# Moving the pieces of the modulation vectors between the stages of a three-block transformer kernel

## The chip, the cores and the metric

The kernel runs on one core of one Trainium2 chip. The metric is the device time of one execution in microseconds (us). Engines are named as in the profile: PE is TensorE, DVE is VectorE, ACT is ScalarE, POOL is GpSimd, SP is SyncE, which here does nothing but issue DMAs.

## The reference, cut to what matters

Two layers with a mixer and a feed-forward network (FFN) each, and then a second block (attention, cross attention, experts), all for 256 tokens of width 1024 in float32. What matters here is the modulation of the first two layers:

```python
def adaln_modulation(c, w, b):                     # w: 1024 x 6144, one per layer
    mod = jax.nn.silu(c) @ w + b
    return [m[:, None, :] for m in jnp.split(mod, N_MOD, axis=-1)]

for layer in range(DEPTH):                         # 2 layers
    shift_m, scale_m, gate_m, shift_f, scale_f, gate_f = adaln_modulation(c, *ada[layer])
    h = rmsnorm(x, pre_m) * (1.0 + scale_m) + shift_m
    x = x + gate_m * rmsnorm(mixers[layer](h), post_m)
    h = rmsnorm(x, pre_f) * (1.0 + scale_f) + shift_f
    x = x + gate_f * rmsnorm(swiglu(h, *ffns[layer]), post_f)
```

The modulations depend on the vector `c` alone, not on the tokens. They can be computed at any time before the place that uses them.

## The kernel before

**Stages.** The program is a list of stages, and every engine walks through it in the same order: `pro`, `proj0`, `ssd`, `mla` (the first layer's mixer), `ffn0`, `mix1`, `gla`, `nsa` (the second layer's mixer), `ffn1`, and then the second block (`mix2` to `experts`). Each engine has its own instruction stream, written out by hand in methods whose names begin with `pe_`, `ve_`, `se_`, `ge_`; the engines wait for each other on semaphores that count finished instructions of a stage.

**Projections.** A projection streams its weights from DRAM as slabs of 128x2048 float32 (1 MB), in a ring of three (`raw`). The products are made of three fp32r matmuls per 128x128 tile (lines 532 to 534; 528 to 530 where the tokens are the stationary side): each weight is split into a high part (`whi`, written by ACT, line 2127) and a low part (`wlo`, a subtraction on DVE or POOL, line 1203). The splits go by blocks of 1024 columns, half a slab, in a ring of three blocks: ACT may cut block j once PE is done with block j-3. `lo_engine` says who makes the low part: in the FFNs blocks with an even number are DVE's and odd ones POOL's; elsewhere in these stages all are POOL's. In `ffn0` DVE's is the first half of every slab. One call of `pe_linear` is one slab: 16 tiles in two halves (j = 0 and 1) of 24 matmuls. Next to it `ve_linear` does what DVE owes that projection, and cuts low parts up to two blocks ahead.

**An FFN** is eleven rounds of a gate slab, an up slab and the down slab of the round before (`pe_ffn`, `ve_ffn`). In each round DVE also multiplies silu(gate) by up (line 1562) and takes the low part of the product (line 1565).

**The modulation pieces.** The first four of the 24 column groups are done in the prologue. The other 80 pieces (list `ADA`: a piece is a quarter of a group of 512 columns) are spread over the program. `ve_ada` does one piece on DVE: it waits for the piece's 128x1024 float32 tile (512 KB, a ring of two, `ada_ring`) and adds its two halves, each times a scalar, to `ada_acc` (lines 1229 and 1232). Four pieces make a group. The call after the fourth one closes the group: there `pe_ada` waits for DVE's fourth piece and sums `ada_acc` over the partitions with four fp32 matmuls, eight records each time (line 617), and `ve_ada` waits for these, writes four columns of `mod_t` (line 1221), and then does its own next piece. Both engines count the calls (`ada_no`), so calls 4, 8, ... 80 close a group. Calls stand at the start of every `pe_linear`, `pe_linear_tok`, and every second column block of `pe_out`; with `eager=True` a projection has two, of which PE makes the second between the two halves of the slab, and DVE makes both before it cuts. `pe_ada` also notes (`ada_slab`) before which weight slab the next piece is loaded; SP issues all loads from one queue, and `sp_ada` waits there for the piece two before.

**Where the calls fall.** `proj0` has 12 (numbers 0 to 11), `ssd` 8, `mla` 8, `ffn0` 22 (28 to 49), `mix1` 5, `gla` 12 including the last `w_nq`, `nsa` 10 (67 to 76), `ffn1` four that do anything (77 to 80). `pe_ada_until` and `ve_ada_until` make up what is missing before a modulation is used; before the change they find nothing to do.

**`mix1` and `gla`.** After the first of four `w_gqk` projections DVE makes a gate and its running sums (four scans, line 1604). In `gla`, seven levels follow each other: DVE and ACT make factors (lines 1626 to 1654), PE a matmul per level (line 883), and between the levels PE fills its time with 11 projections (`FILLS`: 2, 2, 2, 1, 1, 1, 2).

Of the kernel before, what the change touches and what calls it, by code (L numbers as in the profile page):

```python
# [430 lines left out]
    return n, [slice(h0 + p, h0 + p + 2 * n - 1, 2) for h0 in range(0, nh, 2 * n) for p in range(2)]  # L431


ADA = [(0, g, q) for g in range(4, 12) for q in range(4)] + [(1, g, q) for g in range(12) for q in range(4)]


# [49 lines left out]
class Net:  # L486
# [26 lines left out]
    def tensor(self, e):  # L513
        e.wait_ge(self.landed["kc"], 16)
        for stage, run in (("pro", self.pe_pro), ("proj0", self.pe_proj0), ("ssd", self.pe_ssd), ("mla", self.pe_mla),
                           ("ffn0", self.pe_ffn0), ("mix1", self.pe_mix1), ("gla", self.pe_gla), ("nsa", self.pe_nsa),
                           ("ffn1", self.pe_ffn1), ("mix2", self.pe_mix2), ("moba", self.pe_moba), ("xa", self.pe_xa),
                           ("route", self.pe_route), ("gates", self.pe_gates), ("experts", self.pe_experts)):
            self.P.begin(stage)
            run(e)  # L520

    def pe_mm3(self, e, out, tile, xh, xl, start, stop, *keys, moving=False):
# [82 lines left out]
    def pe_ada(self, e):  # L605

        s = self.ada_no["P"]
        if s > len(ADA):
            return
        self.ada_no["P"] += 1  # L610
        self.ada_slab[s] = self.W.due()
        if s and ADA[s - 1][2] == 3:
            layer, g, _ = ADA[s - 1]
            e.wait_ge(*self.at("ada", s - 1))
            ps = self.banks.take(e, "ada", layer, g)
            for j in range(4):
                i = e.matmul(ps[:, j * 128:(j + 1) * 128], self.m.ada_acc[:, j * 128:(j + 1) * 128], self.m.ones, start=True,  # L617
                             stop=True, skip_group_check=True)
            i.then_inc(*self.P(("full", "ada", layer, g)))

    def pe_ada_until(self, e, layer, part):
        while self.ada_no["P"] <= ADA.index((layer, 2 * part + 1, 3)) + 1:
            self.pe_ada(e)
# [57 lines left out]
    def pe_proj0(self, e):  # L681
        m = self.m
        for i in range(3):
            self.pe_linear(e, "w_low", i, 8, 2, m.hH, m.hL, None if i else "mix0", eager=True)
        for i in range(6):
            self.pe_linear(e, "w_xbc", i, 8, 2, m.hH, m.hL)
            if i == 0:
                e.wait_ge(*self.at("low_squares"))
                self.pe_rstd(e, "qa", [range(0, 3)], m.tmp, lambda j: None)
                self.pe_rstd(e, "kva", [range(3, 5)], m.tmp, lambda j: None)  # L690
        e.wait_ge(*self.at("cs"))
        ps = self.banks.take(e, "dt_cs")
        for c in range(2):
            e.transpose(ps[:, 16 * c:16 * c + 16], m.dt[:, c * 128:(c + 1) * 128], m.kc("ident", 0, 16, 16))
            i = e.transpose(ps[:, 32 + 16 * c:48 + 16 * c], m.cs[:, c * 128:(c + 1) * 128], m.kc("ident", 0, 16, 16))
        i.then_inc(*self.P(("full", "dt_cs")))
# [119 lines left out]
    def pe_ffn(self, e, layer):  # L816
        m = self.m
        self.pe_ada_until(e, layer, 4)
        self.P.mark("end", f"mixer{layer}", "P")
        self.pe_norm(e, f"ffn{layer}", True)  # L820
        self.P.mark("sums", f"ffn{layer}", "P")
        for i in range(11):
            self.pe_linear(e, f"w_gate{layer}", i, 8, 2, m.hH, m.hL, None if i else f"ffn{layer}")
            self.pe_linear(e, f"w_up{layer}", i, 8, 2, m.hH, m.hL)
            if i:
                self.pe_down(e, layer, i - 1)
        self.pe_down(e, layer, 10)
        self.pe_post(e, f"ffn{layer}_post", layer, 5)
# [355 lines left out]
    def vector(self, e):  # L1184
        e.wait_ge(self.landed["kc"], 16)
        e.wait_ge(self.landed["pv"], 16)
        for stage, run in (("pro", self.ve_pro), ("proj0", self.ve_proj0), ("ssd", self.ve_ssd), ("mla", self.ve_mla),
                           ("ffn0", self.ve_ffn0), ("mix1", self.ve_mix1), ("gla", self.ve_gla), ("nsa", self.ve_nsa),
                           ("ffn1", self.ve_ffn1), ("mix2", self.ve_mix2), ("moba", self.ve_moba), ("xa", self.ve_xa),
                           ("route", self.ve_route), ("gates", self.ve_gates), ("experts", self.ve_experts)):  # L1190
            self.V.begin(stage)
            run(e)

    def cut_lo(self, e, X, upto):
# [14 lines left out]
    def ve_ada(self, e):  # L1209

        m, V = self.m, self.V
        s = self.ada_no["V"]
        if s > len(ADA):
            return
        self.ada_no["V"] += 1
        if s and ADA[s - 1][2] == 3:
            layer, g, _ = ADA[s - 1]
            c0 = 48 * layer + 4 * g
            ps = self.banks.tile("ada", layer, g)
            e.wait_ge(*self.at("full", "ada", layer, g))  # L1220
            e.tensor_tensor(out=m.mod_t[:, c0:c0 + 4], in0=ps[:, :].rearrange("p (a n) -> p a n", a=4)[:, :, 0],
                            in1=m.pv(f"ada_b{layer}", 4 * g, 4), op=ALU.add).then_inc(*V(("out", "ada", layer, g)))
        if s < len(ADA):
            _, _, q = ADA[s]
            e.wait_ge(self.ada_landed[s % 2], 16 * (s // 2 + 1))
            for k in range(2):
                c, w = m.silu_c[:, 2 * q + k:2 * q + k + 1], m.ada_ring[:, s % 2, k * 512:(k + 1) * 512]
                if q == 0 and k == 0:
                    e.tensor_scalar(out=m.ada_acc, in0=w, scalar1=c, scalar2=None, op0=ALU.mult).then_inc(*V())
                else:  # L1230
                    e.wait_ge(*V.last)
                    e.scalar_tensor_tensor(out=m.ada_acc, in0=w, scalar=c, in1=m.ada_acc, op0=ALU.mult,  # L1232
                                           op1=ALU.add).then_inc(*V(*([("ada", s)] if k else [])))
# [163 lines left out]
    def ve_proj0(self, e):  # L1397
        m, V = self.m, self.V
        e.memset(m.xb[:, :, 0:3], 0.0).then_inc(*V(("xb_zero",)))
        for i in range(3):  # L1400
            self.ve_linear(e, "w_low", i, 8, 2, eager=True)
            if i == 1:
                e.wait_ge(*self.at("out", "w_low", 1))
                e.tensor_scalar(out=m.dtx, in0=m.kp[0:16, :], scalar1=m.pv("dt_bias", rows=16), scalar2=None,
                                op0=ALU.add).then_inc(*V(("dt_raw",)))
# [137 lines left out]
    def ve_ffn(self, e, layer):  # L1543
        m, V = self.m, self.V
# [9 lines left out]
            e.wait_ge(*self.at("end", f"mixer{layer}", eng))  # L1554
        for i in range(11):
            s = slice(2 * (i % 2), 2 * (i % 2) + 2)
            self.ve_linear(e, f"w_gate{layer}", i, 8, 2)
            self.ve_linear(e, f"w_up{layer}", i, 8, 2)
            e.wait_ge(*self.at("out", f"w_gate{layer}", i))
            e.wait_ge(*self.at("full", f"w_up{layer}", i))  # L1560
            pu = self.banks.tile(f"w_up{layer}", i)[:, 0:512].rearrange("p (a t) -> p a t", a=2)
# [1498 lines left out]
```

## Time and profile before

| what | value |
|---|---|
| median of 3 runs | 2291.11 us (2288.9 to 2291.63) |
| the profiled execution | 2293.22 us, its span 2291.1 us |
| PE busy | 2033.5 us (89%) |
| DVE busy | 1311.9 us (57%) |
| ACT busy | 978.7 us (43%) |
| POOL busy | 1112.1 us (49%) |
| mean granted TensorE clock | 0.947 |

The stages stand in the trace at these times of the span: `proj0` from about 50 us, `ssd` from 131, `mla` from 192, `ffn0` from 292, `mix1` from 510, `gla` from 557, `nsa` from 714, `ffn1` from 850 to 1060. Busy time counts overlapping matmuls once; an idle stretch is given in brackets with what ended it. PEclk is the TensorE clock granted, as a share of full speed.

### The profile page before, as it was taken

Reading aid. Unit: us, or ns where it says so; the run is one execution under the profiler, and the core shown is the slowest. Engines: PE = TensorE matmul, PEld = TensorE weight load, DVE = VectorE, ACT = ScalarE, POOL = GpSimd, SP = SyncE. Lnnn points to the kernel's source line nnn. Section 1 sums busy time; section 2 is a strip of 40 time slices with the busy share of each in tenths; the row PEclk is TensorE's granted clock in tenths of the full one; section 3 lists DMA queues with packets and bytes.
Section 4 is the critical chain, followed back from the end, with each engine's and each line's share of the span. In section 5 each row is a group of like instructions: output and inputs, shape, how many; then the busy total and the mean of one; then the engine's idle time right before and its main releaser. Section 6 shows DMA issues by size and latency. Waiting matters only on the chain.

```text
span 2291.1 us, 38041 instructions
## 1 busy us (share of the span) xinstructions
PE 2033.5 (89%) x15708; PEld 1957.5 (85%) x15708; DVE 1311.9 (57%) x2049; ACT 978.7 (43%) x1433; POOL 1112.1 (49%) x506
## 2 busy tenths in 40 slices
PE   6688889987889769997988889767999999999998
PEld 6676789977877659997988879756899999999998
DVE  5788755537774764333823448999744444444444
ACT  5334354444333334444443545356334444444443
POOL 2452344445543233444856657866744444444443
PEclk8889899997889799999989989999999999999999
DMA  7542446644445234554434334322456555555543
GB/s 278 193 168 92 181 159 237 234 174 149 166 151 189 83 102 160 183 182 152 166 110 148 129 111 164 131 88 79 162 205 218 184 219 216 184 183 182 184 183 129
DMA packets 75915, 378.43 MB, mean 165 GB/s; under 512 B 6976, under 2 KB 24528, under 8 KB 38496
## 3 DMA queue, kind: packets, MB, share of 16 engines
q1 hardware_dynamic: 75744, 376.00, 45.6%
q8 instruction: 125, 2.05, 0.4%
q14 instruction: 46, 0.38, 0.0%
HBM read 366.54 MB, written 9.44 MB: 164 GB/s over the span
## 4 chain that ended last, share of the span: by engine, by line
PE 65%; DVE 20%; POOL 4%; ACT 3%; issue 2%; DMA 1%; DVEq 0%; SPq 0%; ACTq 0%
PE ps L532 19%; PE ps L533 18%; PE ps L534 18%; POOL wlo L1203 4%; DVE arena L1232 3%; PE ps L581 2%; DVE arena L1329 1%; DVE rs_t L2063 1%; DVE arena L1654 1%; DVE arena L2035 1%; PE ps L617 1%; ACT whi L2127 1%; PE ps L760 1%; DVE small L1317 1%; DVE arena L2063 1%
## 5 line engine op out<-in xcount | busy, mean ns | idle before, releaser
L1203 POOL TENSOR_TENSOR wlo<-raw,whi 128x1024 fp32r<-128x1024 f32 x387 | 979.2, 2538 | 1013.5 <-ACT whi L2127 1012.3
L532 PE MATMUL ps<-hhi,whi 128*128 128x256 f32 x2696 | 787.9, 292 | 70.7 <-POOL wlo L1203 30.5
L2127 ACT ACTIVATE whi<-raw 128x1024 fp32r<-128x1024 f32 x559 | 587.9, 1056 | 594.5 <-PE ps L534 470.9
L533 PE MATMUL ps<-hlo,whi 128*128 128x256 f32 x2696 | 778.4, 289 | 0.0
L534 PE MATMUL ps<-hhi,wlo 128*128 128x256 f32 x2696 | 777.4, 288 | 0.0
L532 PEld LDWEIGHTS ps<-hhi,whi 128*128 128x128 f32 x2696 | 533.6, 198 | 81.5 <-issue 49.9
L533 PEld LDWEIGHTS ps<-hlo,whi 128*128 128x128 f32 x2696 | 534.4, 198 | 0.1
L534 PEld LDWEIGHTS ps<-hhi,wlo 128*128 128x128 f32 x2696 | 533.5, 198 | 0.0
L532 PE MATMUL ps<-chi,whi 128*128 128x256 f32 x1600 | 457.6, 286 | 15.0 <-DVE clo L2091 7.2
L533 PE MATMUL ps<-clo,whi 128*128 128x256 f32 x1600 | 454.8, 284 | 0.0
L534 PE MATMUL ps<-chi,wlo 128*128 128x256 f32 x1600 | 454.7, 284 | 0.0
L1203 DVE TENSOR_TENSOR wlo<-raw,whi 128x1024 fp32r<-128x1024 f32 x172 | 217.4, 1264 | 396.9 <-ACT whi L2127 396.9
L532 PEld LDWEIGHTS ps<-chi,whi 128*128 128x128 f32 x1600 | 309.0, 193 | 19.3 <-issue 9.5
L533 PEld LDWEIGHTS ps<-clo,whi 128*128 128x128 f32 x1600 | 309.2, 193 | 0.0
L534 PEld LDWEIGHTS ps<-chi,wlo 128*128 128x128 f32 x1600 | 309.2, 193 | 0.0
L1232 DVE SCALAR_TENSOR_TENSOR arena<-arena,gs_t 128x512 f32<-128x512 f32 x140 | 181.1, 1294 | 14.6 <-DMA arena<-in_ada 5.8
L2584 ACT ACTIVATE rs_t<-ps 128x256 f32<-128x256 f32 x106 | 40.8, 385 | 164.7 <-PE ps L534 163.3
L581 PE MATMUL ps<-arena,kc_t 128*128 128x256 f32 x250 | 66.5, 415 | 27.4 <-ACT arena L2166 24.5
L2035 POOL TENSOR_TENSOR arena<-arena 128x512 f32<-128x512 f32 x48 | 72.4, 1511 | 30.7 <-PE ps L1157 15.4
L581 PEld LDWEIGHTS ps<-arena,kc_t 128*128 128x128 f32 x250 | 49.2, 206 | 41.5 <-issue 12.2
L1157 PE MATMUL ps<-rs_t,arena 128*128 128x128 f32 x344 | 49.1, 292 | 25.6 <-issue 11.5
L617 PE MATMUL ps<-kc_t,arena 128*128 128x128 f32 x160 | 29.6, 344 | 47.3 <-DVE arena L1232 45.7
(368 smaller groups left out, 2197.4 us busy)
## 6 DMA issues: line engine op xcount, KB each, us to landing
raw<-in_peer_down SPq DMA_DIRECT2D x64, 1024.0 KB, 4.8
raw<-in_peer_up SPq DMA_DIRECT2D x64, 1024.0 KB, 7.2
arena<-in_ada SPq DMA_DIRECT2D x80, 512.0 KB, 4.4
raw<-in_w_gate SPq DMA_DIRECT2D x22, 1024.0 KB, 4.9
raw<-in_w_up SPq DMA_DIRECT2D x22, 1024.0 KB, 4.9
raw<-in_w_down SPq DMA_DIRECT2D x22, 1024.0 KB, 4.8
arena<-in_ada SPq DMA_DIRECT2D x8, 1024.0 KB, 14.9
raw<-in_w_gab SPq DMA_DIRECT2D x8, 1024.0 KB, 4.7
```

The lines of the kernel that those rows point to most:

```text
L532: e.matmul(out, hi, xh, start=start, stop=False, skip_group_check=True)
L533: e.matmul(out, hi, xl, start=False, stop=False, skip_group_check=True)
L534: i = e.matmul(out, lo, xh, start=False, stop=stop, skip_group_check=True)
L581: i = e.matmul(ps[:, gi * 256:gi * 256 + T], self.m.ones, sq[:, j, :], start=n == 0, stop=n == len(tiles) - 1, skip_group_check=True)
L617: i = e.matmul(ps[:, j * 128:(j + 1) * 128], self.m.ada_acc[:, j * 128:(j + 1) * 128], self.m.ones, start=True, stop=True, skip_group_chec ...
L1157: t = e.matmul(ps[:, i * 128:(i + 1) * 128], m.oh1[:, n % 3, i * 128:(i + 1) * 128], m.oh2[n % 3][:, i * 128:(i + 1) * 128], start=True, s ...
L1203: e.tensor_tensor(out=lo, in0=w, in1=hi.bitcast(F32), op=ALU.subtract).then_inc(*X(("lo", j)))
L1232: e.scalar_tensor_tensor(out=m.ada_acc, in0=w, scalar=c, in1=m.ada_acc, op0=ALU.mult, op1=ALU.add).then_inc(*V(*([("ada", s)] if k else [])))
L2035: e.tensor_tensor(out=m.oh1[:, n % 3, :].rearrange("p (t a b) -> p t a b", t=4, a=8), in0=bc(ta[:, sl, :].unsqueeze(3), [128, 4, 8, 16]), ...
L2063: e.tensor_tensor(out=m.oh2[n % 3].rearrange("p (t n) -> p t n", t=4), in0=bc(m.iota.unsqueeze(1), [128, 4, 128]), in1=bc(m.pk[:, 2, 4 * n ...
L2127: e.activation(hi, w, ACT.Copy, scale=1.0).then_inc(*self.A(("hi", j)))
L2584: e.activation(m.ge[:, i, :] if i < NST else m.co[:, i % 2, :], self.banks.tile("expert", i)[:, 0:T], ACT.Gelu_apprx_tanh, scale=1.0).then ...
```

## The change

The calls are placed by stage. The first projection of the program (`w_low`, three slabs) has one call per slab and no longer two. Gate and up projections of both FFNs get two calls each. A limit by stage, `ADA_UPTO`, ends the calls in `mix1`, `gla` and `nsa` after number 72.

```diff
+ADA_UPTO = {"mix1": 72, "gla": 72, "nsa": 72}
 ...
             self.P.begin(stage)
+            self.ada_upto = ADA_UPTO.get(stage, len(ADA))
             run(e)
 ...
         s = self.ada_no["P"]
-        if s > len(ADA):
+        if s > self.ada_upto:
             return
 ...
-            self.pe_linear(e, "w_low", i, 8, 2, m.hH, m.hL, None if i else "mix0", eager=True)
+            self.pe_linear(e, "w_low", i, 8, 2, m.hH, m.hL, None if i else "mix0")
 ...
-            self.pe_linear(e, f"w_gate{layer}", i, 8, 2, m.hH, m.hL, None if i else f"ffn{layer}")
-            self.pe_linear(e, f"w_up{layer}", i, 8, 2, m.hH, m.hL)
+            self.pe_linear(e, f"w_gate{layer}", i, 8, 2, m.hH, m.hL, None if i else f"ffn{layer}", eager=True)
+            self.pe_linear(e, f"w_up{layer}", i, 8, 2, m.hH, m.hL, eager=True)
```

The same four edits are made on DVE's side (`vector`, `ve_ada`, `ve_proj0`, `ve_ffn`). Counted through, the calls now fall so: `proj0` 9 (0 to 8), `ssd` 8 (9 to 16), `mla` 8 (17 to 24), `ffn0` 44 (25 to 68), `mix1` 4 (69 to 72), `gla` and `nsa` none, `ffn1` 8 (73 to 80). Groups close at the same numbers as before, so at other places.

## Rows read from the trace of the kernel before

**Rows 1.** The page's part 4: the chain that ended last, by engine.
```profile
PE 65%; DVE 20%; POOL 4%; ACT 3%; issue 2%; DMA 1%; DVEq 0%; SPq 0%; ACTq 0%
```
**Rows 2.** Stretches: length, busy us of PE, PEld, DVE, ACT, POOL, PEclk, DMA.
```profile
292.00:500.00 208.00, 201.66 (x1643) 199.97 (x1643) 101.94 (x117) 91.70 (x109) 86.80 (x39) 0.98 0.61 220
565.00:660.00 95.00, 66.82 (x506) 65.93 (x505) 78.90 (x68) 30.09 (x35) 52.00 (x19) 0.86 0.44 165
```
**Rows 3.** Waits of PE, 290 to 900 us, then 60 to 290: total, times, longest.
```profile
PE ps L617 <- DVE arena L1232: 24.9, 5, 8.7
...
PE ps L617 <- DVE arena L1232: 20.8, 3, 8.3
```
**Rows 4.** DVE's timeline in `ffn0`, rounds with and without a closing: start, length.
```profile
402.98 0.16 DVE L1221 TENSOR_TENSOR mod_t<-ps,pv_t 128x4 f32<-128x4 f32 x1 [3.02 <-PE ps L617]
403.06 0.48 DVE L1229 TENSOR_SCALAR arena<-arena,gs_t 128x512 f32<-128x512 f32 x1
...
404.24 1.22 DVE L1203 TENSOR_TENSOR wlo<-raw,whi 128x1024 fp32r<-128x1024 f32 x1
...
418.23 3.57 DVE L1232 SCALAR_TENSOR_TENSOR arena<-arena,gs_t 128x512 f32<-128x512 f32 x2
421.73 1.21 DVE L1203 TENSOR_TENSOR wlo<-raw,whi 128x1024 fp32r<-128x1024 f32 x1
423.04 1.54 DVE L1232 SCALAR_TENSOR_TENSOR arena<-arena,gs_t 128x512 f32<-128x512 f32 x2
```
**Rows 5.** The timelines of PE, ACT and POOL in the same rounds.
```profile
401.89 1.06 PE L617 MATMUL ps<-kc_t,arena 128*128 128x128 f32 x8
...
414.30 0.28 PE L532 MATMUL ps<-chi,whi 128*128 128x256 f32 x1
...
411.68 1.06 ACT L2127 ACTIVATE whi<-raw 128x1024 fp32r<-128x1024 f32 x1 [1.82 <-PE ps L534]
...
412.82 2.40 POOL L1203 TENSOR_TENSOR wlo<-raw,whi 128x1024 fp32r<-128x1024 f32 x1 [3.36 <-ACT whi L2127]
...
418.58 2.68 POOL L1203 TENSOR_TENSOR wlo<-raw,whi 128x1024 fp32r<-128x1024 f32 x1 [3.36 <-ACT whi L2127]
```
**Rows 6.** DMA, 395 to 432 us: rate in 40 slices; issue to landing.
```profile
GB/s 292 0 0 97 248 434 412 412 115 80 239 425 403 270 283 0 44 133 434 425 115 0 44 168 363 425 381 328 0 89 221 425 421 407 137 80 239 425 372 27
...
arena<-in_ada SPq DMA_DIRECT2D x4, 512.0 KB, 5.6
```
**Rows 7.** PE's timeline at closings, a level and restarts, in order of time.
```profile
131.25 0.55 PE L532 MATMUL ps<-hhi,whi 128*128 128x256 f32 x1 [1.33 <-POOL wlo L1203]
...
156.34 2.07 PE L617 MATMUL ps<-kc_t,arena 128*128 128x128 f32 x8 [6.01 <-DVE arena L1232]
...
536.07 2.08 PE L617 MATMUL ps<-kc_t,arena 128*128 128x128 f32 x8
...
557.29 2.05 PE L883 MATMUL ps<-arena 128*128 128x128 f32 x16 [0.69 <-ACT arena L2139]
...
573.55 2.08 PE L617 MATMUL ps<-kc_t,arena 128*128 128x128 f32 x8 [8.46 <-DVE arena L1232]
```
**Rows 8.** PE's timeline after the levels, in `nsa`, and at its last projection.
```profile
673.10 3.09 PE L892 MATMUL ps<-raw,hT_t 128*128 128x24 f32 x27
...
767.06 0.79 PE L999 MATMUL ps<-arena 128*128 128x128 f32 x2 [3.07 <-DVE arena L1771]
...
835.66 1.16 PE L617 MATMUL ps<-kc_t,arena 128*128 128x128 f32 x8 [2.40 <-DVE arena L1232]
```
**Rows 9.** DVE's timeline: `mla`, the scans of `mix1`, a level of `gla`.
```profile
253.11 7.13 DVE L1232 SCALAR_TENSOR_TENSOR arena<-arena,gs_t 128x512 f32<-128x512 f32 x4
...
544.53 11.04 DVE L1604 TENSOR_TENSOR_SCAN arena<-arena 128x256 f32<-128x256 f32 x4
...
636.27 0.69 DVE L1626 TENSOR_TENSOR arena<-arena 128x512 f32<-128x512 f32 x1
...
647.22 0.69 DVE L1626 TENSOR_TENSOR arena<-arena 128x512 f32<-128x512 f32 x1
```

More of the change, by code:

```diff
@@ L1191, in vector @@
             self.V.begin(stage)
+            self.ada_upto = ADA_UPTO.get(stage, len(ADA))
             run(e)
@@ L1212, in ve_ada @@
         s = self.ada_no["V"]
-        if s > len(ADA):
+        if s > self.ada_upto:
             return
@@ L1400, in ve_proj0 @@
         for i in range(3):
-            self.ve_linear(e, "w_low", i, 8, 2, eager=True)
+            self.ve_linear(e, "w_low", i, 8, 2)
             if i == 1:
@@ L1556, in ve_ffn @@
             s = slice(2 * (i % 2), 2 * (i % 2) + 2)
-            self.ve_linear(e, f"w_gate{layer}", i, 8, 2)
-            self.ve_linear(e, f"w_up{layer}", i, 8, 2)
+            self.ve_linear(e, f"w_gate{layer}", i, 8, 2, eager=True)
+            self.ve_linear(e, f"w_up{layer}", i, 8, 2, eager=True)
             e.wait_ge(*self.at("out", f"w_gate{layer}", i))
```

## The prediction

> **What bounds the kernel now.** I read the chain first, then the busy time by stage, then who waits for whom. The chain is 65% PE and 20% DVE [rows 1], so some stages are PE's and some are DVE's. `ffn0` is PE's: busy 201.66 of 208 us, DVE only 101.94 [rows 2]. `gla` is DVE's: DVE 78.90 of 95 us, PE 66.82 [rows 2]. Moving pieces from the second kind of stage to the first looks free. The waits tell where the pieces hurt: PE stood 24.9 us in five closings after 290 us and 20.8 us in three before, each up to 8.7 us long, because a closing waits for DVE's piece [rows 3]. So I follow two things: where DVE has time for a piece, and where PE meets a closing.
>
> One fact decides the prices. A pair of `ada_acc` instructions takes 1.54 us, but 3.57 us where POOL cuts a block beside it [rows 4]. In that case POOL's cut started at 418.58, during the first of the two, and took 2.68 us instead of 2.40; the second instruction came out only at 421.73 [rows 4, 5]. So DVE and POOL take turns at something, instruction by instruction, and whoever has waited goes next.
>
> The sum is made against the profiled execution: 2293.2 us, its span 2291.1, the median of the runs also 2291.1.
>
> **`proj0` to `mla`, three pieces fewer: about 0.** Five groups close here, all elsewhere than before.
> - `proj0`: the closings in `w_low` 2 and `w_xbc` 2 go, where PE stood (two of the three waits in the 20.8 us; the longest is 8.3) [rows 3]. New ones stand at `w_xbc` 1 and 5. The second finds its piece long done. The first waits for DVE, which comes late from `dt`. I get PE through `w_xbc` about 9 us earlier (bounds: 4, and 14.8, the two waits whole).
> - `ssd`: the closing at 156.34 with its wait of 6.01 us [rows 7] becomes two inside slabs, in `w_z` 1 and 3. PE stops halfway, and DVE's second piece must wait for it before the decays: +3 (0 to 6).
> - `mla`: closing 20 now falls between the third and fourth slab of `w_out0a`. DVE reaches piece 19 only after the softmax, at 253.11. With one wait for POOL the pair ends about 256.6; then 2.1 us of closing and a slab started cold (5.8 + 1.5), then the transposes (1.9): DVE copies at about 268.7, where it did after 253.11 + 7.13 = 260.2 and 1.3 us of copying [rows 9]. +7; the closing ahead of `w_out0b` shrinks by about 1.2. Net +6 (2 to 9).
>
> Sum 0 (-8 to +8).
>
> **`ffn0`, 44 calls for 22: +29.** DVE's time is no problem: two more pairs per gate and up come to 22 x (1.54 to 3.57) = 34 to 79 us against 106 idle. The order inside the round is. PE's matmuls follow each other at 201.66/1643 = 0.12 us [rows 2], a slab of 48 takes 5.76, a round 17.28. The first group to close is at call 28, the second call of `w_up` 0, and then every round closes one in the middle of its up slab: 11 closings, where there were six at the head of a gate. A closing takes PE 0.9 us: 414.30 - 401.89 = 12.41, less two slabs [rows 5]. So 5 x 0.9 = +4.5.
>
> Now the place. Let U be the moment when PE has done the first half of the up slab; in the trace it is 414.30 - 2.88 = 411.42. ACT starts the next high part at U+0.26 and POOL its cut at U+1.40 [rows 5]. DVE writes `mod_t` 1.09 after the closing began (402.98 against 401.89) [rows 4, 5], so at U+1.09, its first half-piece runs from U+1.17 to U+1.65, and POOL, waiting since U+1.40, goes next. From there the trace has the same pattern: first instruction done at 418.98, cut done at 422.94 [rows 4], 3.96 us. So the low part of the down slab's first half, which DVE cuts after the piece, is ready at U+5.6. PE wants it at U + 0.9 + 2.88 = U+3.8. PE waits 1.9 us, eleven times: +21. Without POOL in the way the cut would end at U + 1.09 + (405.46 - 402.98) = U+3.57, just in time [rows 4]. Bounds: 0 and 1.9 + 2.4, one more turn of POOL.
>
> The other three pieces fit: piece 3 of a round must be done at U for the closing, and I get U-0.6 if its tile has landed. That load is issued after the first piece, some 7 us before U, and takes 5.6 [rows 6]. The Trainium skill (SBUF — State Buffer, "Summary: rules for kernel authors") reckons about 358 GB/s for such transfers; by it the tile, behind a slab of 1 MB, would land later and each closing wait some 0.3 us more, +3 in all. The trace moves 434 GB/s in its fastest slices [rows 6], so I leave that out.
>
> A stop can also cost clock: after 1.33 us idle the first matmul took 0.55 us (the 1.2 GHz level) [rows 7], after 2.40 us the closing took 1.16, the full level [rows 8]. A slab that restarts cold lasts 1.5 us longer. One in four gives 11 x 0.25 x 1.5 = +4 (0 to 16). `ffn0`: 4.5 + 21 + 4, +29 (+4 to +50).
>
> **`mix1` and `gla`: -17.** Closing 72 stands ahead of `w_gqk` 2, and piece 71 comes on DVE behind the scans (544.53, 11.04 us) [rows 9]. Before, PE passed its closing at 536.07 and had all of `w_gqk` done for the level at 557.29 [rows 7]. Now it stops after `w_gqk` 1, at 543, until DVE has done the pair at 557, closes (2.1), and does two slabs (11.5 + 1.5 cold): the first level starts at about 572.7, +15. The scans hid no PE stop before; this is the largest loss here. Then the closings in `w_gv`, `w_gg` and `w_ncd` are gone, and with them waits of 8.46 (at 573.55) [rows 7], 8.7 and 5 us (of the 24.9) [rows 3], three times 2.1 us, and 16 instructions of pieces on DVE. PE's own floor from 572.7 is 7 levels x 2.05 [rows 7] + 11 slabs x 5.76 = 77.7, to 650.4. In levels 3 to 6 DVE leads: its period was 647.22 - 636.27 = 10.95 [rows 9], 9.4 without the 1.54 of the pair, against PE's 7.8. I get line 892 at 655.6 and not 673.10 [rows 8]: -17.5. Bounds: -22.7 (PE's floor) and -11 (levels keep 10.95, POOL taking the freed turns).
>
> **`nsa`: -6.4.** Closing 68 goes (-0.9, PE alone bounds there); the pair ahead of the wait of 3.07 at 767.06 [rows 8] gives 2.0; around `w_out1b` the wait of 2.40 and the closing of 1.16 [rows 8] go, -3.5. The others lie beside PE or DVE work. Bounds -9 and -3.
>
> **`ffn1`: +2.5.** Two closings instead of one. Blocks have the other parity here: DVE cuts the second halves, so its cut is due 2.9 us later and closing 76 costs 0.9. At 80 the piece before it is late by its load: 1.6. Bounds 0 and +6.
>
> **Sum:** 0 + 29 - 17.5 - 6.4 + 2.5 = +7.6, a profiled execution of about 2301 and a median of about 2299 us.
>
> **Rivals.**
> - *The closings in `ffn0` don't stop PE* (DVE keeps its turn for the two instructions, or POOL's cut comes after them). For it: U+3.57 is before U+3.8, and U+1.17 and U+1.40 are 0.23 us apart. Against: 3.57 us for the pair whenever POOL had asked [rows 4]. Then +29 becomes +4.5 and the kernel is faster: 2291 - 17 = 2274.
> - *The second mixer gives back less.* The stop of PE behind the scans spreads, and the levels keep their 10.95: `gla` -11, `mla` at its worst +3. For it: DVE's two-input instructions there often wait for POOL anyway. 2299 + 10 = 2309. With every stop of `ffn0` cold as well, 2320. This is on the forecast's side.
> - *The early mixer gains and `gla` reaches PE's floor:* -7 and -5 more, `ffn0`'s stops as forecast: 2287, faster or level.
> - *The pieces don't move as counted.* The call numbers are fixed by the program, so I give this nothing.
>
> **How the numbers follow.** Within 0.2% means 4.6 us, about what a measurement of this kernel can tell from no change. Forecast 0.47 (2289 to 2307: 0.37 slower, 0.10 level); no stops 0.25 (faster); less given back 0.13 (slower); early gain 0.15 (0.07 faster, 0.08 level). So slower 0.50, same 0.18, faster 0.32. The range takes in the first rival and the second: 2272 to 2317.
>
> **What would show it.** In `ffn0`: DVE line 1229 followed by a line 1232 of about 2.8 us, PE waiting for DVE's `wlo` (line 1203) about 1.9 us in each of 11 rounds, a round of about 20.1 us, `ffn0` some 25 to 30 us longer. PE idle about 14 us ahead of a closing near 557, then a `gla` without any wait of line 617, ended by line 892 some 17 us earlier against the stage's start. In `mla` a closing that waits about 8 us. I am wrong if PE's `ffn0` stays at 17.3 us plus 0.9 per round, or if PE doesn't stop at `w_gqk` 2.

## The result, and the profile after

| | kernel before | changed kernel |
|---|---|---|
| median | 2290.36 us (2288.9 to 2291.63, 4 runs) | 2313.65 us (2310.65 to 2316.88, 4 runs) |
| profiled execution, span | 2293.2, 2291.1 us | 2311.63, 2309.8 us |

The ratio is 1.0102, 95% interval 1.0085 to 1.012: slower by 1%, where 2299 was forecast (2272 to 2317). The rise is 23.3 us by the medians and 18.7 us by the spans of the two profiled executions; the stages below add up to the second.

The chain of the changed kernel (shares of the span by engine, then by line) has an entry that [rows 1] hadn't: the load of a piece's tile.

```profile
PE 59%; DVE 25%; DMA 5%; POOL 4%; ACT 4%; issue 2%; SPq 0%; DVEq 0%; ACTq 0%
```

To see where the time went I cut both spans at the same marks: the second batch of sums in each RMS norm (line 581 before, 583 after), the first matmul of the first level (line 883, now 885) and the last projection's (line 892, now 894). Each row is one stretch: its length, then busy time (and instructions) of PE, PEld, DVE, ACT and POOL, granted clock, DMA share and GB/s. First the kernel before, then the changed one.

```profile
287.40:505.22 217.82, 208.51 (x1665) 205.15 (x1665) 107.77 (x131) 96.77 (x119) 90.05 (x43) 0.98 0.58 211
505.22:557.29 52.07, 42.91 (x248) 38.61 (x249) 36.13 (x39) 25.87 (x39) 29.26 (x17) 0.77 0.21 73
557.29:673.10 115.81, 87.63 (x664) 86.62 (x665) 96.99 (x84) 36.91 (x43) 60.82 (x24) 0.87 0.44 163
673.10:845.68 172.58, 142.17 (x972) 122.88 (x971) 97.96 (x188) 63.06 (x134) 50.64 (x27) 0.86 0.41 147
845.68:1060.80 215.12, 202.41 (x1625) 198.42 (x1625) 81.59 (x88) 96.79 (x119) 88.69 (x43) 0.98 0.47 165
```

```profile
290.12:541.98 251.86, 217.22 (x1705) 209.31 (x1705) 154.30 (x180) 96.72 (x119) 92.58 (x43) 0.98 0.63 229
541.98:606.02 64.04, 43.15 (x248) 38.46 (x248) 34.04 (x44) 25.92 (x40) 28.72 (x17) 0.79 0.28 101
606.02:694.30 88.28, 80.51 (x640) 79.77 (x641) 73.75 (x51) 36.99 (x43) 62.14 (x24) 0.94 0.35 121
694.30:856.11 161.81, 134.51 (x949) 116.91 (x947) 69.88 (x162) 63.04 (x134) 48.68 (x27) 0.88 0.33 117
856.11:1078.90 222.79, 205.10 (x1633) 200.85 (x1633) 91.29 (x97) 96.78 (x119) 89.10 (x43) 0.98 0.48 168
```

The differences, beside the forecast's terms:

| stage | measured | forecast |
|---|---|---|
| up to `ffn0` (287.40 to 290.12) | +2.7 | 0 |
| `ffn0` | +34.0 | +29 |
| `mix1` to the first level | +12.0 | +15 |
| levels (`gla`) | -27.5 | -32.5 |
| `nsa` | -10.8 | -6.4 |
| `ffn1` | +7.7 | +2.5 |
| all that follows | +0.6 | 0 |
| sum | +18.7 | +7.6 |

(The forecast's -17.5 for `mix1` and `gla` is split here as it was worked: +15, then the rest.) In `ffn0` PE's busy time rose by only 8.7 of the 34 us. The rest is waiting, and the waits of that stretch name it (engine and line waited for: us in total, times, longest; line 1235 is the second and further instructions of a piece, line 1232 the first of a group, line 1206 a low part, line 619 the closing):

```profile
DVE arena L1235 <- DMA arena<-in_ada: 50.0, 20, 4.7
PE ps L534 <- DVE wlo L1206: 18.0, 12, 2.6
PE ps L619 <- DVE arena L1235: 5.7, 9, 1.4
```

None of the three is among the waits of the same stretch before. One round shows how they hang together. DVE with POOL's cut, then SP's issues, then PE:

```profile
365.60 1.22 DVE L1206 TENSOR_TENSOR wlo<-raw,whi 128x1024 fp32r<-128x1024 f32 x1
371.51 1.54 DVE L1235 SCALAR_TENSOR_TENSOR arena<-arena,gs_t 128x512 f32<-128x512 f32 x2 [4.70 <-DMA arena<-in_ada]
374.30 0.17 DVE L1224 TENSOR_TENSOR mod_t<-ps,pv_t 128x4 f32<-128x4 f32 x1 [1.25 <-PE ps L619]
374.38 1.24 DVE L1232 TENSOR_SCALAR arena<-arena,gs_t 128x512 f32<-128x512 f32 x1
375.65 0.75 DVE L1235 SCALAR_TENSOR_TENSOR arena<-arena,gs_t 128x512 f32<-128x512 f32 x1
376.32 1.22 DVE L1206 TENSOR_TENSOR wlo<-raw,whi 128x1024 fp32r<-128x1024 f32 x1
372.96 2.38 POOL L1206 TENSOR_TENSOR wlo<-raw,whi 128x1024 fp32r<-128x1024 f32 x1 [3.35 <-ACT whi L2130]
```

```profile
364.42 0.33 SPq L2832 DMA_DIRECT2D raw<-in_w_gate  x1
364.79 1.25 SPq L2843 DMA_DIRECT2D arena<-in_ada  x2
369.69 0.33 SPq L2832 DMA_DIRECT2D raw<-in_w_up  x1
```

```profile
373.11 1.16 PE L619 MATMUL ps<-kc_t,arena 128*128 128x128 f32 x8 [1.38 <-DVE arena L1235]
377.69 0.35 PE L534 MATMUL ps<-chi,whi 128*128 128x256 f32 x1 [0.55 <-DVE wlo L1206]
```

PE wants to close at 371.73, the middle of the up slab. The fourth piece's tile has just landed: its load was the first of the two issued right behind the gate slab's 1 MB, at 364.79, and took 6.7 us (the other, at 365.71, is the next piece's: it had waited for the piece that DVE ended at 365.68). So PE stops 1.38 us. Then DVE writes `mod_t`, does the next piece, and only then the cut that PE wants for the down slab: a second stop. POOL's cut has begun before DVE's piece; the first of the piece's two instructions, a multiply, takes 1.24 us where it takes 0.48 alone, and ends 0.28 us after POOL's cut.

The round shown has the longest of the late closings. This is a more usual one:

```profile
414.15 2.40 POOL L1206 TENSOR_TENSOR wlo<-raw,whi 128x1024 fp32r<-128x1024 f32 x1 [3.35 <-ACT whi L2130]
414.65 2.18 DVE L1232 TENSOR_SCALAR arena<-arena,gs_t 128x512 f32<-128x512 f32 x1
416.86 0.75 DVE L1235 SCALAR_TENSOR_TENSOR arena<-arena,gs_t 128x512 f32<-128x512 f32 x1
```

Here PE stops 0.46 us for the closing and 1.49 us for the cut. In nine of the eleven closings POOL's cut begins ahead of both instructions, as here, and the multiply takes 1.24 to 2.25 us. Only in the first two does it come between them, as forecast (0.48, then 2.77 us). In the nine rounds that have both stops they add up to 1.93 to 1.96 us each time.

From the second round on a round takes (521.65 - 336.29)/9 = 20.60 us, measured from one line 1565 (was 1562) to the next, against 17.77 before.

In the mixer PE stops for piece 71 behind the scans, and ahead of the first level, as forecast; `ffn1` has a stop that was not forecast in this size (both views end soon after the start, so they show four of the eight records):

```profile
590.18 1.22 PE L619 MATMUL ps<-kc_t,arena 128*128 128x128 f32 x4 [8.45 <-DVE arena L1235]
898.49 0.71 PE L619 MATMUL ps<-kc_t,arena 128*128 128x128 f32 x4 [3.88 <-DVE arena L1235]
```

### The profile page after: what moved, and what is told of

The parts are those of the page before. It is cut to its first block, busy times and chain, and to the rows that moved or that the text cites. A ratio compares the mean times of both kernels' runs of the same rounds, so it can differ in the third digit from the quotient of the medians.

```text
span 2309.8 us, 38040 instructions
## 1 busy us (share of the span) xinstructions
PE 2033.7 (88%) x15708; PEld 1953.7 (85%) x15708; DVE 1310.6 (57%) x2049; ACT 978.8 (42%) x1433; POOL 1113.2 (48%) x506
## 4 chain that ended last, share of the span: by engine, by line
PE 59%; DVE 25%; DMA 5%; POOL 4%; ACT 4%; issue 2%; SPq 0%; DVEq 0%; ACTq 0%
PE ps L534 17%; PE ps L535 16%; PE ps L536 16%; DMA arena<-in_ada 5%; DVE arena L1235 4%; POOL wlo L1206 4%; PE ps L583 2%; DVE arena L1332 1%; DVE rs_t L2066 1%; ACT whi L2130 1%; DVE arena L1657 1%; PE ps L619 1%; DVE arena L1232 1%; DVE arena L2038 1%; DVE arena L1282 1%
## 5 line engine op out<-in xcount | busy, mean ns | idle before, releaser
L1235 DVE SCALAR_TENSOR_TENSOR arena<-arena,gs_t 128x512 f32<-128x512 f32 x140 | 160.9, 1149 | 58.4 <-DMA arena<-in_ada 51.0
L2094 DVE TENSOR_TENSOR clo<-rs_t,chi 128x256 fp32r<-128x256 f32 x128 | 71.2, 556 | 4.4
## 6 DMA issues: line engine op xcount, KB each, us to landing
arena<-in_ada SPq DMA_DIRECT2D x8, 1024.0 KB, 15.5
```

The costliest lines, as they stand in the source:

```text
L2094: e.tensor_tensor(out=m.cL[:, s, :], in0=w, in1=m.cH[:, s, :].bitcast(F32), op=ALU.subtract).then_inc(*V(("weighed", i)))
```

## The experiments

Eleven kernels, five rounds each. e1 to e7 are the changed kernel with one edit; e9 builds on e4, e11 on e9; e8 and e10 combine edits. The last column is the ratio times 2291 us, less the same for the changed kernel (2314.4). The changed kernel was timed in a set of its own, and each ratio is known to 2 to 4 us either way, so I take that column as good to some 5 us. The profiled executions give the same differences 1 to 6 us smaller in size.

| kernel | median | ratio to before, 95% | against the changed kernel |
|---|---|---|---|
| e1_head | 2288.28 | 0.9979 (0.9968 to 0.999) | -28 |
| e2_cut_first | 2295.90 | 1.0013 (1.0004 to 1.0022) | -20 |
| e3_close_later | 2300.77 | 1.0040 (1.0027 to 1.0052) | -14 |
| e4_three_tiles | 2305.11 | 1.0056 (1.0043 to 1.0069) | -11 |
| e5_no_limit | 2306.71 | 1.0060 (1.0046 to 1.0073) | -10 |
| e6_parity | 2310.85 | 1.0091 (1.0077 to 1.0105) | -3 |
| e7_ffn1_single | 2306.29 | 1.0059 (1.0046 to 1.0073) | -10 |
| e8_combined | 2266.35 | 0.9889 (0.9874 to 0.9905) | -49 |
| e9_tiles_earlier | 2310.70 | 1.0079 (1.0065 to 1.0093) | -5 |
| e10_best | 2257.18 | 0.9850 (0.9833 to 0.9866) | -58 |
| e11_pool_after | 2285.69 | 0.9976 (0.9967 to 0.9986) | -29 |

And by stage, between the marks of above, from the profiled executions, with the round of `ffn0`. Each row is one execution. How far such numbers repeat is shown by the last column, which no edit touches (1228.8 to 1231.0), and by `ffn0` in the changed kernel, e3, e5 and e7, where it has the same code (251.9 to 256.1):

| | `ffn0` | round | `mix1` | levels | `nsa` | `ffn1` | rest |
|---|---|---|---|---|---|---|---|
| before | 217.8 | 17.77 | 52.1 | 115.8 | 172.6 | 215.1 | 1230.3 |
| changed | 251.9 | 20.60 | 64.0 | 88.3 | 161.8 | 222.8 | 1230.9 |
| e1 | 247.6 | 20.20 | 46.3 | 88.5 | 162.1 | 222.7 | 1231.0 |
| e2 | 239.5 | 19.21 | 63.1 | 87.6 | 162.1 | 223.5 | 1228.8 |
| e3 | 251.9 | 20.60 | 51.9 | 89.7 | 162.4 | 223.5 | 1228.8 |
| e4 | 253.9 | 20.66 | 57.9 | 87.6 | 161.5 | 222.3 | 1230.1 |
| e5 | 253.3 | 20.60 | 64.0 | 95.2 | 161.9 | 213.2 | 1228.9 |
| e6 | 252.1 | 20.47 | 62.9 | 87.6 | 161.3 | 222.7 | 1231.0 |
| e7 | 256.1 | 20.89 | 62.8 | 88.3 | 161.9 | 215.9 | 1231.0 |
| e8 | 234.4 | 18.85 | 48.2 | 87.4 | 163.5 | 216.0 | 1230.1 |
| e9 | 251.2 | 20.53 | 64.5 | 88.4 | 161.9 | 222.3 | 1230.2 |
| e10 | 224.2 | 18.12 | 48.1 | 88.8 | 159.5 | 215.9 | 1229.2 |
| e11 | 226.8 | 18.18 | 63.0 | 88.4 | 162.0 | 222.2 | 1230.1 |

### e1_head: the three extra calls in `w_low` back

```diff
-            self.pe_linear(e, "w_low", i, 8, 2, m.hH, m.hL, None if i else "mix0")
+            self.pe_linear(e, "w_low", i, 8, 2, m.hH, m.hL, None if i else "mix0", eager=True)
-            self.ve_linear(e, "w_low", i, 8, 2)
+            self.ve_linear(e, "w_low", i, 8, 2, eager=True)
```

> The changed kernel with one part undone: the three w_low projections before the first FFN take two calls each again. 28 calls then stand before ffn0 where there were 25, so each group of four closes at the head of a gate slab and no longer in the middle of an up slab, and closing 72 comes at the head of the second layer's mixer, ahead of the scans. Pieces in ffn0: as many as in the changed kernel. Theory (it is the place of the closing that stops PE): the 1.4 us wait for the down slab's low part and the 0.7 us wait for the fourth piece go, a round falls from 20.4 to between 18.2 and 19.2 (at the gate's head DVE has two pieces in front of the up slab's cut, which may cost 0.8), ffn0 -15; the stop of 8.5 us at w_gqk 2 goes, with its closing of 2.1, and what of it DVE doesn't take back later is worth -8; in all 2313.6 - 26 = 2288 (2280 to 2296). Rival (it is the number of pieces in ffn0 that costs, by DVE's time and the loads): the round stays at 20 us and only the mixer gains: 2305.

The total came out as the theory had it, but not by its parts. `mix1` lost its stop: 64.0 to 46.3, and the levels after it kept all of that (88.5). `ffn0` gained only 4.3 of 15. But for the first, the closings don't wait any more; yet PE still stops ahead of the down slab. DVE, POOL, PE:

```profile
386.52 3.18 DVE L1235 SCALAR_TENSOR_TENSOR arena<-arena,gs_t 128x512 f32<-128x512 f32 x4 [2.79 <-DMA arena<-in_ada]
389.61 3.40 DVE L1206 TENSOR_TENSOR wlo<-raw,whi 128x1024 fp32r<-128x1024 f32 x1
389.44 2.50 POOL L1206 TENSOR_TENSOR wlo<-raw,whi 128x1024 fp32r<-128x1024 f32 x1 [3.36 <-ACT whi L2130]
393.17 0.36 PE L534 MATMUL ps<-chi,whi 128*128 128x256 f32 x1 [2.09 <-DVE wlo L1206]
```

Two pieces, the first of them held 2.79 us by its load, stand in front of the cut, and the cut then runs into POOL's (3.40 us for 1.22). So it wasn't the closing that made PE stop there; what costs is a piece between a cut and its use.

### e2_cut_first: the cut between the two pieces of an up slab

```diff
         self.ve_ada(e)
+        if eager and name == "w_up0":
+            self.ve_cuts(e, name, (i + 1) * nn * kt - 1)
         if eager:
             self.ve_ada(e)
```

> The changed kernel, but in the up slabs of ffn0 DVE takes its cut (the low part of the down slab's first half) between the slab's two pieces and not behind both; PE's closings stay in the middle of the up slab. Theory (PE's stop ahead of the down slab is the wait for this cut, which stands behind the piece that takes turns with POOL): the cut is done 1.2 us after its high part, the wait of 1.4 us goes in each of 11 rounds, round 20.4 to 19.0, 2313.6 - 15 = 2298 (2294 to 2303). Rival (PE would meet the next late thing, POOL's cut or the act tiles, so that the stop only moves): round stays above 20, 2309 or more.

The theory holds: the round is 19.21, and of PE's waits for DVE's cut in `ffn0` one is left, in the first rounds. What remains are the closings' waits for the late fourth piece (7.4 us in 9).

### e3_close_later: closing 72 after the levels

```diff
-ADA_UPTO = {"mix1": 72, "gla": 72, "nsa": 72}
+ADA_UPTO = {"mix1": 71, "gla": 71, "nsa": 72}
```

> The changed kernel, but closing 72 is held back from the mixer's w_gqk 2 to the stage nsa (limit 71 in mix1 and gla). Theory: PE's idle 8.5 us and the closing of 2.1 us ahead of w_gqk 2 go, the first level starts 12 us earlier, and since PE ran without a gap through the first five levels most of it is kept: -9, and the closing costs 1 in nsa: 2313.6 - 8 = 2305.5 (2301 to 2310). Rival (DVE and POOL bound the levels whatever PE does, so the stop was hidden): the levels' last matmul comes no more than 2 us earlier, 2312.

`mix1` is 12.1 us shorter (51.9), the levels are 1.4 longer and `nsa` 0.6. So 10.1 of the 12.1 us are kept, where I had expected 8 of 12: most of the stop was on the path.

### e4_three_tiles: three tiles for the pieces

```diff
-        self.ada_acc, self.ada_ring = alloc(512), alloc(2048, 2, 1024)
+        self.ada_acc, ring = alloc(512), alloc(2048, 2, 1024)
+        self.ada_tiles = [ring[:, 0, :], ring[:, 1, :], self.arena[:, NARENA - 1024:NARENA]]
...
+ADA_SLOT = [s % 2 if s < 24 else s % 3 for s in range(80)]
```

> The changed kernel with three tiles for the pieces' loads in place of two from piece 24 on (the third in a part of the arena that is free from the end of ssd to the levels). Theory (the fourth piece of a group is late because its load can only be issued when the second piece is done, and takes 5.7 us): DVE's waits for loads in ffn0 (47.9 us) nearly go, the closings' waits of 0.4 to 1.4 us (7 in all) go, and in ffn1 the stop of 3.9 and part of the one of 1.5: 2313.6 - 11 = 2303 (2299 to 2307). Rival (the load is late because the queue is full, whatever is issued earlier): the waits stay, 2313.

In `ffn0` the theory fell: DVE's waits for loads stayed, and so did the round.

```profile
DVE arena L1237 <- DMA arena<-in_ada: 48.7, 18, 5.2
```

```profile
406.98 0.33 SPq L2834 DMA_DIRECT2D raw<-in_w_gate  x1
407.36 0.91 SPq L2849 DMA_DIRECT2D arena<-in_ada  x2
412.27 0.33 SPq L2834 DMA_DIRECT2D raw<-in_w_up  x1
```

SP has a tile to fill at once now (0.91 us for the two issues, 1.25 before), but both loads still go out behind the gate slab, since their place in SP's order is the slab that was due when PE made the call. The time that this execution gained lies in `mix1` (57.9 for 64.0), and it can't be put down to the third tile: PE's busy time there is 38.1 us for 43.2 over the same work, at a granted clock of 0.85 for 0.79. A wait of 3.4 us for `w_gk`'s load is gone too, but the closing's wait is 2.2 longer.

### e9_tiles_earlier: three tiles, and each load one slab earlier

```diff
-        self.ada_slab[s] = self.W.due()
+        self.ada_slab[s] = self.W.due() - (s >= 24)
```

> The changed kernel with three tiles for the pieces' loads, and from piece 24 on each load is issued one weight slab earlier. With three tiles alone DVE's waits for loads in ffn0 stayed (48.7 against 47.9 us): two loads still went out together behind the gate slab's 1 MB (issues at 406.98, 407.36 and the next, landed at 413.2). Theory (the order of issue makes the load late, 1 MB at 434 GB/s is 2.4 us): DVE's waits for loads fall below 20 us, the closings' waits in ffn0 (6.2 us) go, ffn0 -6, and something of ffn1's stops; against the three tiles' 2305 this is 2298 (2294 to 2302). Rival (the queue is busy all the time, an earlier piece only makes a slab later, and PE or ACT waits for that): within 2 of 2305 or above.

By its time the rival holds (2310.7), but not by its reason. The loads are in time now: no wait for `in_ada` nor of a closing is left in `ffn0`'s waits. But the round is 20.53 on average: 20.20 in seven of the nine, and 21.68 in two, whose granted clock is 0.92 and not 1.00. Nearly all of the stop has moved to the cut. DVE, POOL, PE:

```profile
414.54 0.48 DVE L1234 TENSOR_SCALAR arena<-arena,gs_t 128x512 f32<-128x512 f32 x1
415.05 2.77 DVE L1237 SCALAR_TENSOR_TENSOR arena<-arena,gs_t 128x512 f32<-128x512 f32 x1
417.74 1.21 DVE L1208 TENSOR_TENSOR wlo<-raw,whi 128x1024 fp32r<-128x1024 f32 x1
414.76 2.51 POOL L1208 TENSOR_TENSOR wlo<-raw,whi 128x1024 fp32r<-128x1024 f32 x1 [3.04 <-ACT whi L2132]
419.10 0.36 PE L536 MATMUL ps<-chi,whi 128*128 128x256 f32 x1 [1.81 <-DVE wlo L1208]
```

PE's waits for this cut are 22.5 us in 12, ten of them 1.81 us long. This is the mechanism of the forecast in its pure form (it had 1.9), here in all eleven closings: POOL's cut comes in ahead of the piece's second instruction, which ends at 417.82, after the cut's end at 417.27. In the changed kernel the late load splits nearly the same loss (1.95 us) into two stops, and POOL's cut holds the first instruction.

### e11_pool_after: the same, POOL's cut behind DVE's

```diff
                 e.wait_ge(*self.at("hi", j))
+                if who == "G" and self.W.blocks[j][0] == "w_down0":
+                    e.wait_ge(*self.at("lo", j - 1))
```

> The kernel with three tiles and earlier loads, whose rounds in ffn0 hold one stop of PE, 1.81 us in each, for DVE's cut ahead of the down slab; here POOL's cut of the down slab's second half waits until DVE's cut of the first half is done, so that it no longer starts in the middle of DVE's piece. Order and number of DVE's instructions stay. Theory (DVE and POOL take turns: the piece's second instruction lasted 2.77 us beside POOL's cut and 0.75 without): the pair is done 2.0 us earlier, DVE's cut 0.3 before PE wants it, the stop goes, POOL's cut ends 0.7 before its own use: 10 to 11 times 1.8, 2310.7 - 19 = 2292 (2288 to 2296). Rival (the piece in front of the cut costs PE the time, beside POOL or not; or the stop moves to POOL's cut): 2305 or more.

This isolates the turns. Not one of DVE's instructions is moved:

```profile
404.25 0.47 DVE L1236 TENSOR_SCALAR arena<-arena,gs_t 128x512 f32<-128x512 f32 x1
404.76 0.75 DVE L1239 SCALAR_TENSOR_TENSOR arena<-arena,gs_t 128x512 f32<-128x512 f32 x1
405.43 1.22 DVE L1210 TENSOR_TENSOR wlo<-raw,whi 128x1024 fp32r<-128x1024 f32 x1
406.79 2.41 POOL L1210 TENSOR_TENSOR wlo<-raw,whi 128x1024 fp32r<-128x1024 f32 x1 [5.38 <-DVE wlo L1210]
```

The second instruction takes 0.75 instead of 2.77 us, the round 18.18 instead of 20.53, the kernel 2285.7. A round is now the 17.28 us of its 144 matmuls and one closing of 0.9; the rest of the 9.0 us over the kernel before (226.8 for 217.8) lies in the first rounds. The gain of 25 us is more than the 19 that I had put down for the stops: each had also cost PE some 0.2 us of busy time at its restart, and e9's two rounds at the lower clock 1.5 each. POOL waits 53.9 us for it in ten rounds, and PE has no stop for a low part from POOL that e9 hadn't (0.4 us in all in both). The Trainium skill (SBUF — State Buffer, "SBUF: two separate sides") says that VectorE and GpSimd hold a shared pair of ports as an exclusive lock, for a whole instruction, when VectorE reads two operands from SBUF or runs in a mode that uses both ports; whoever starts first has it. This pair of runs agrees with it: 415.05 + 2.77 is POOL's end plus 0.55.

### e6_parity: POOL cuts the first halves in `ffn0`, DVE the second

```diff
-            return ("V", "G")[j % 2]
+            return ("G", "V")[j % 2] if name[-1] == "0" else ("V", "G")[j % 2]
```

> The changed kernel with the halves swapped between DVE and POOL in the first FFN's slabs: DVE cuts the second half of each, POOL the first. The closings stay in the middle of the up slab. Theory (PE's 1.4 us stop ahead of the down slab is for DVE's cut behind a piece that takes turns with POOL): DVE's cut is now due 2.9 us later, and POOL's, which has nothing in front, is in time: the stop goes, the closing's own 0.7 stays, a round 20.4 to 19.0, 2313.6 - 15 = 2298 (2294 to 2303). Rival (who cuts doesn't matter, since the two take turns and POOL's cut is delayed as much by the piece): a stop of 1 or more stays, now for POOL, 2309 or more.

The rival is nearer, though not for its reason. The wait for the cut is gone; the closings now wait 23.6 us where they waited 5.7:

```profile
PE ps L619 <- DVE arena L1235: 23.6, 11, 3.9
```

In one round, for example, DVE's fourth piece lands late as before (1.22 us waited) and now takes 2.88 us for 1.54, beside POOL's cut. The turn-taking hit another instruction, on which PE waits as well.

### e5_no_limit: no limit in the mixer

```diff
-ADA_UPTO = {"mix1": 72, "gla": 72, "nsa": 72}
+ADA_UPTO = {}
```

> The changed kernel without the limit of 72 in the second layer's mixer: pieces 72 to 79 come in gla again, with closings 76 and 80 between the levels, and ffn1 has none; closing 72 stays at w_gqk 2. Theory (a closing in gla stops PE for a piece that DVE reaches late): from line 885's first to line 894 the kernel before took 115.8 us with three closings and the changed one 88.3 with none, 9.2 each; two closings cost 18; ffn1 loses its two closings and their stops, -8.8; in all 2313.6 + 9 = 2323 (2317 to 2328). Rival (the levels of the kernel before were slow by the six or more pairs on DVE and POOL's turns and not by the closings' stops, or the gain lay elsewhere): the levels cost 4 or less more, 2309 or less.

My theory fell. Two closings and eight pieces in the levels cost 6.9 us (88.3 to 95.2), not 18 (the rival had 4 or less), and `ffn1` without them gains 9.6. The two closings (each view ends after some of the eight records):

```profile
621.94 0.72 PE L619 MATMUL ps<-kc_t,arena 128*128 128x128 f32 x5
654.54 0.71 PE L619 MATMUL ps<-kc_t,arena 128*128 128x128 f32 x4 [1.21 <-DVE arena L1235]
```

Before, the levels' closings stood 8.46 us [rows 7], 8.71 and 5.10 us for their piece. The 27.5 us that the levels gave back were thus mostly the places of three closings (22.3 us of waits, against 1.2 for two here; the kernel before also had four more pieces there, which no run takes out alone), and the limit itself, given the other edits, loses more in `ffn1` (9.6) than it brings in the levels (6.9).

### e7_ffn1_single: one call per projection in `ffn1`

```diff
-            self.pe_linear(e, f"w_up{layer}", i, 8, 2, m.hH, m.hL, eager=True)
+            self.pe_linear(e, f"w_up{layer}", i, 8, 2, m.hH, m.hL, eager=layer == 0)
```

(and the same for `w_gate` and on DVE)

> The changed kernel with one call per projection in the second FFN again and two only in the first: the last eight pieces lie over four rounds of ffn1 and not over two; closings 76 and 80 come at the head of an up slab. Theory (ffn1 lost 7.7 us because two pieces in a slab wait for their loads, so that the closings stand 1.5 and 3.9 us, and PE restarts cold): ffn1 -6, 2307.5 (2305 to 2310). Rival (the closings themselves or the loads among the slabs cost it): within 1.5 of 2313.

As the theory had it: `ffn1` 222.8 to 215.9, with one closing's wait of 0.3 us left. Two closings cost as good as nothing there; two pieces in one slab cost 7. The whole profiled execution is only 4.1 us shorter, since `ffn0`, which this edit leaves alone, took 4.2 longer, with two rounds of 21.70 and 22.10 us at a granted clock of 0.92.

### e8_combined and e10_best

The edits of e1, e2 and e7 together, and then those of e9 on top.

> The changed kernel with three edits together: two calls again for w_low (closings at the head of a gate, closing 72 ahead of the scans), DVE's cut in the up slabs of ffn0 between the slab's two pieces, one call per projection in ffn1. With the first edit alone PE still stood 2.0 to 2.6 us in each round of ffn0, because DVE waited 2.8 us for the third piece's load, then did two pieces (3.2) and came with its cut into POOL's (3.40 for 1.22), while the cut's high part had been ready since 386.48 of that trace. Theory (the cut behind the pieces, not the number of pieces, is what is left in ffn0): a round falls from 20.4 to 18.3, 10 of them -20, ffn1 -6, from 2288.3 to 2262 (2257 to 2270), faster than the kernel before by over 1%. Rival (four pieces in a round cost PE 3 us wherever they stand): only ffn1's share, 2282.

> The three edits together (closings at a gate's head and ahead of the scans, the cut between the pieces, one call per projection in ffn1), with three tiles and loads one slab earlier as well. In the three edits' trace PE's rounds in ffn0 are 18.17 us, which is 144 matmuls and one closing, with three stops left (3.35, 2.19 and 1.35 us), two of them behind late loads. Theory (the loads decide these stops): 2266 - 4 = 2262 (2259 to 2265). Rival (the loads are off PE's path now): 2266 or more.

e8 came out as its theory had it (2266 for 2262, its average round 18.85 for 18.3). For e10 the direction holds, but 2257 lies below its range (2259 to 2265): it gained 9 us by the medians, more than the three stops, 4.0 of them in `nsa` by the two profiled executions, where the stops aren't. Its rounds in `ffn0` are 144 matmuls and a closing without any idle time, 18.17 us apart:

```profile
352.02 0.72 PE L621 MATMUL ps<-kc_t,arena 128*128 128x128 f32 x5
370.18 0.61 PE L621 MATMUL ps<-kc_t,arena 128*128 128x128 f32 x4
388.35 0.72 PE L621 MATMUL ps<-kc_t,arena 128*128 128x128 f32 x5
```

So two pieces for each projection of the first FFN and none in the levels is worth 1.5% against the kernel before, when the pieces are placed right: `ffn0` +6.4, `mix1` -4.0, levels -27.0, `nsa` -13.1 us. The same plan with its places left to chance was 1% slower.

## Why the prediction was right, and where its sizes were off

- **Direction and largest term: right.** The time lies in the range, near its upper end: the rise is 18.7 us in the profiled pair where 7.6 was forecast. `ffn0` +34.0 for +29. That DVE's piece and POOL's cut take turns, and that the down slab's low part is late by it, is shown by e9 (1.81 us of stop for 1.9) and e11 (without POOL's cut beside the piece the stop is gone, -25 us by the medians of the two). But the sign that I had named, line 1232 followed by a line 1235 of about 2.8 us (there 1229 and 1232), is in two of the eleven closings only. In the others the closing came late, POOL's cut was first, and the multiply waited. That both orders cost PE about the same (1.95 and 1.81 us) was luck.
- **The round: 20.6 for 20.1.** It is 17.28 for the matmuls, 0.9 for the closing, 1.95 for the two stops, and 0.47 of PE's busy time at the two restarts (18.65 us busy, 18.18 in e11's rounds), which I had not priced.
- **The clock in `ffn0`: +4 for "one in four" cold slabs, and there was none.** In the changed kernel's execution all ten intervals between rounds have a granted clock of 1.00. The size of one was right: e9's two rounds at 0.92 are 1.48 us longer. How many an execution has is not shown to follow from the change: e7, with the same `ffn0`, has two among the nine, e3 and e5 none. So the sum for `ffn0` came close with one term too many and the restarts and the late load left out.
- **"Piece 3 of a round must be done at U", U - 0.6 "if its tile has landed":** it had not. By the forecast's own numbers (issued 7 us before U, 5.6 us long, then 1.54 us for the pair) the piece is done at U + 0.1. It went out 6.9 us before U, behind the gate slab only, and took 6.7 us in the round shown, where the piece is done 1.3 us after U, and 5.8 in the more usual one, where it is done 0.4 after. That gave 5.7 us of closings' waits in the stage. By the rule of the Trainium skill that I left out (SBUF — State Buffer, "Summary: rules for kernel authors") I would have had 0.3 us for each closing; 5.7 us over 11 is 0.5, so its size is nearer than the nothing that I took. No run here tells whether it is the rate that makes it. But as e9 shows, taking the lateness away saves 0.4 us in a round (20.20 for 20.60), since the stop at the cut grows from 1.4 to 1.8: the two were mostly one loss.
- **`mix1`: right in place, a little large in size.** The first level came 12.0 later, not 15: DVE had the piece at 590.13, 8.45 us after PE stopped, not 14. Against the start of the stage PE stopped 2.0 us later than forecast and DVE was done 3.6 earlier: the four scans took 6.56 us and not 11.04. POOL's cuts ran beside them only up to 586.78, since PE's stop left POOL no more to cut; before they ran beside them all the time. In e3, where PE doesn't stop, the scans take 11.04 again. e3 gets the 12.1 back.
- **Levels: -27.5 for -32.5;** with `mix1` -15.5 for -17.5, inside the bounds. Through the first five levels PE doesn't wait at all. Then it waits 3.11 us for line 1647 and 4.32 us for POOL's `wlo` at 686.29, and the slab after that takes 8.0 us for 5.8, at a granted clock of 0.69. These 9.7 us on PE's floor of 77.7 make 87.4 of the 88.3 measured, where I had put 82.9 between the two marks (the 5.2 above the floor are not worked out in the forecast; three single-slab levels at 9.4 for 7.8 give 4.8). The reason I gave for the gain (closings' waits of 8.46, 8.7 and 5 us gone) is what e5 points to, and their 22.3 us of waits are most of the 27.5; what the pairs on DVE count for is not shown alone.
- **`nsa`: -10.8, beyond the bound of -9.** The three terms of the forecast are there: -1.05 up to line 643 at 750.40 for -0.9, -1.9 from there to the end of the wait at 767.06 for -2.0, and -3.5 from 810.53 on for -3.5. What it lacked is the clock. Behind the wait of 3.07 us the same 73 matmuls had run at a granted clock of 0.52, the 1.2 GHz level; behind a wait of 0.87 us they run at 1.00, and take 5.6 us less, of which 1.2 goes into a longer wait for DVE right after. (In the 15 to 17 us ahead of them, wait included, the clock was 0.70 before and 0.68 in the changed kernel.) Before, then changed:

```profile
767.06:780.20 13.14, 13.14 (x73) 10.16 (x73) 3.46 (x12) 0.91 (x2) 0.00 (x0) 0.52 0.32 120
785.32:792.90 7.58, 7.58 (x73) 5.99 (x74) 2.27 (x8) 0.91 (x2) 0.00 (x0) 1.00 0.41 141
```

- **`ffn1`: +7.7, beyond the bound of +6.** I gave closing 80 a wait of 1.6 us for its load and it was 3.88, and closing 76 stood 1.45. e7 shows that the doubled calls are the cause (-6.9). The change doubled them there too; I had priced only two closings.
- **Up to `ffn0`: +2.7 for 0.** Within its bounds, and its parts were smaller than forecast. In `ssd`, at line 736 (before 734), PE was 2.2 us ahead, not 6; from there on it lost 4.9, not 6. The closing in `mla` waited 7.0 us, near the forecast 8.
- **The rival with the second mixer giving back less** (2309) was near the result by its number, not its story: `mix1`, levels and `nsa` together gave back 2.4 us more than forecast, and the 11.1 us between +7.6 and +18.7 are 2.7 up to `ffn0`, 5.0 in `ffn0`, 5.2 in `ffn1` and 0.6 behind it, less those 2.4. Without the clock in `nsa` the second mixer would have given back 2 us less than forecast. The first rival (closings don't stop PE) is out.

## What to carry to other kernels

Work slipped into an engine's gaps is priced by its place in that engine's order, not by its length: ask what stands behind it, who waits for that, and when its own input lands. 44 pieces in the same stage cost 34, 17 or 6 us according to where the cut, the closing and the load stood. When a wait for one late thing is taken away, look at what the next one was: with loads in time PE waited nearly as long (1.81 us for 1.95 in a round), at another line. And a wait taken away can be worth more than its length, where the matmuls behind it had run at the lower clock.

## What the runs showed of the hardware that I had not expected

- A single wait on POOL, 53.9 us of idle time in ten rounds, made the kernel 25 us faster. With a two-operand subtraction of 128x1024 on POOL beside it, a DVE instruction of 0.75 us took 2.77, and a cut of 1.22 us took 3.40; the multiply of the piece, with one large operand, took 1.24 to 2.25 where it takes 0.48 alone.
- Two loads of 512 KB issued behind a 1 MB slab landed 5.8 to 7.0 us after their issue in the changed kernel and 5.8 to 6.6 in e4, which had a free tile earlier (in two rounds of the first and one of the second). In e9, with the loads one slab earlier in the order of the program, DVE has no wait for them in `ffn0`.
- Of nine rounds of the same matmuls in e9, seven took 20.20 us at a granted clock of 1.00 and two 21.68 at 0.92, each with the same stop of 1.81 us.
